# Two-part-size FFN: parts of 576, 768 and 768 tokens in place of three of 704, and the first weight blocks prepared during the out projection

## The reference

```python
def block_out(x, pool_o, attn_o, w_out, norm_ffn, w_gate, w_up, w_down):
    h = x + jnp.concatenate([pool_o, attn_o], axis=-1) @ w_out
    hn = rms_norm(h, norm_ffn)
    return h + (jax.nn.silu(hn @ w_gate) * (hn @ w_up)) @ w_down
```

## Time and profile before

| | before |
|---|---|
| median of three runs | 2101.21 us (2101.12 to 2104.17) |
| profiled execution | 2103.07 us, its span 2101.3 us |
| PE busy | 2075.9 us, 99% of the span |
| PE weight loads | 1885.5 us |
| DVE / ACT / POOL busy | 1277.1 / 884.0 / 777.9 us |
| mean granted clock of PE | 0.997 |
| DMA | 212.89 MB, mean 101 GB/s |

### The profile page before, as it was taken

One profiled execution on the slowest core, in us unless ns is written; L12 is line 12 of the kernel. 1 busy time (PEld: TensorE's weight loads), 2 busy tenths in 40 slices (PEclk: granted clock), 3 DMA queues, 4 the chain that ended last, 5 costly groups with the idle time before them and its releaser, 6 DMA issues.

```text
span 2101.3 us, 33467 instructions
## 1 busy us (share of the span) xinstructions
PE 2075.9 (99%) x12470; PEld 1885.5 (90%) x12470; DVE 1277.1 (61%) x2070; ACT 884.0 (42%) x2149; POOL 777.9 (37%) x503
## 2 busy tenths in 40 slices
PE   8999999999999999999999999999999999999999
PEld 7888888877888899999998999999998999999997
DVE  5655555553222566766666766766667767666665
ACT  6766666653334533333333433333334333333331
POOL 0000000034324544354435653445445643544352
PEclk9999999999999999999999999999999999999999
DMA  7011111033774532333224523333224422222222
GB/s 189 29 41 41 39 39 41 24 101 112 219 243 148 171 108 89 110 106 109 78 77 151 189 88 108 108 106 90 95 81 159 161 81 70 72 81 72 70 80 75
DMA packets 243401, 212.89 MB, mean 101 GB/s; under 512 B 21149, under 2 KB 220618, under 8 KB 243242
## 3 DMA queue, kind: packets, MB, share of 16 engines
q1 hardware_dynamic: 243242, 210.76, 32.6%
HBM read 170.03 MB, written 40.79 MB: 100 GB/s over the span
## 4 chain that ended last, share of the span: by engine, by line
PE 93%; ACT 2%; DVE 1%; issue 1%; SPq 1%; DMA 1%; POOL 0%; DVEq 0%; ACTq 0%; POOLq 0%
PE ps L813 27%; PE ps L815 27%; PE ps L814 27%; PE ps L914 2%; PE ps L888 2%; PE ps L1030 1%; PE ps L900 1%; PE ps L832 1%; SPq L466 1%; PE ps L1032 1%; PE ps L1028 1%; PE ps L876 1%; ACT s_sb L1208 1%; PE ps L931 1%; PE ps L940 0%
## 5 line engine op out<-in xcount | busy, mean ns | idle before, releaser
L746 POOL TENSOR_TENSOR w_lo<-w_lo_raw,w_hi 128x512 fp32r<-128x512 f32 (+1 forms) x240 | 393.3, 1645 | 606.5 <-PE ps L815 412.7
L813 PE MATMUL ps<-xs_hi,w_hi 128*128 128x352 f32 x1848 | 596.5, 323 | 3.6 <-POOL w_lo L746 2.8
L815 PE MATMUL ps<-xs_lo,w_hi 128*128 128x352 f32 x1848 | 597.8, 324 | 0.0
L813 PEld LDWEIGHTS ps<-xs_hi,w_hi 128*128 128x128 f32 x1848 | 347.6, 188 | 5.7 <-POOL w_lo L746 3.1
L815 PEld LDWEIGHTS ps<-xs_lo,w_hi 128*128 128x128 f32 x1848 | 351.0, 190 | 0.0
L1718 DVE TENSOR_TENSOR h<-ps,h 128x512 f32<-128x512 f32 (+1 forms) x396 | 270.3, 688 | 118.4 <-PE ps L815 112.1
L814 PE MATMUL ps<-xs_hi,ws_lo 128*128 128x352 f32 x1056 | 339.6, 322 | 0.0
L746 POOL TENSOR_TENSOR ws_lo<-ws_lo_raw,w_hi 128x512 fp32r<-128x512 f32 x204 | 295.3, 1449 | 112.2 <-DVE ws_lo_raw L1561 68.4
L1275 ACT ACTIVATE w_hi<-ws_lo_raw 128x512 fp32r<-128x512 f32 x264 | 165.5, 628 | 326.2 <-DVE ws_lo_raw L1561 326.0
L813 PE MATMUL ps<-w_hi,act_hi 128*128 128x512 f32 x660 | 257.2, 390 | 2.6 <-DVE act_lo L1641 2.6
L814 PE MATMUL ps<-w_hi,act_lo 128*128 128x512 f32 x660 | 256.9, 389 | 0.0
(11 more groups left out here) (142 smaller groups left out, 3248.0 us busy)
## 6 DMA issues: line engine op xcount, KB each, us to landing
w_lo_raw<-in_w_gate SPq DMA_DIRECT2D x66, 512.0 KB, 5.1
w_lo_raw<-in_w_up SPq DMA_DIRECT2D x66, 512.0 KB, 5.2
w_lo_raw<-in_w_down SPq DMA_DIRECT2D x66, 512.0 KB, 4.1
xload<-in_x_prompt SPq DMA_DIRECT2D x16, 512.0 KB, 4.2
mix_d<-o_st SPq DMA_DIRECT2D x64, 128.0 KB, 1.8
xt_lo_raw<-mix_d SPq DMA_DIRECT2D x16, 512.0 KB, 6.0
wg_hi_raw<-in_x_prompt SPq DMA_DIRECT2D x16, 512.0 KB, 5.1
h_d<-wg_hi_raw SPq DMA_DIRECT2D x16, 512.0 KB, 2.6
```

Source lines behind the costliest of these rows:

```text
L746: nc.gpsimd.tensor_tensor(lo, raw, hi.bitcast(F32), ALU.subtract).then_inc(done, 1)
L813: nc.tensor.matmul(out, s_hi, m_hi, start=first, stop=False, skip_group_check=partial)
L815: return nc.tensor.matmul(out, s_hi, m_lo, start=False, stop=final, skip_group_check=partial)
```

## The change

1. The parts are 576, 768 and 768 tokens: 4.5, 6 and 6 tiles, NB = 288, 384 and 384. Only the first part has a half tile; the last part's last tile holds 64 prompt and 64 sample rows and is stored in two transfers.
2. High and low row blocks lie in one tensor, `xs`, of 14 slots. Because of the sizes, part 0's low block 6 lies in the ends of slots 3 to 5, so that from block 3 on `rows_high(1, m)` waits for product (21, 6).
3. The high part of weight block 0, and the sum that is block 1, get a place of their own (`first_hi`, `first_s3`). `weight_sum(0, 0)`, `high2(0, 0)` and `low2(0, 0)` run at tiles 8, 9 and 10 of the out projection; `rows_high` and `first_rows_low` of part 0 run a tile earlier.
4. ACT's last step of the out projection is ordered anew, and both `stage_copy` of the last tile, with their `x_transposes` on PE, move to later: the transposes behind products (0, 4) and (0, 6) (they were behind 2 and 4), the copies behind gates 0 and 2.
5. SP issues `load_gate_up(2)` ahead of `load_down(0)` and the last `store_hn`; it was behind both.
6. At the end of part 0, `rows_low(1, 3)` and `rows_low(1, 4)` run together, since there is one tile less.

**ACT, around the end of the out projection.** Before: (`w_hi<-` rows are `high2`; `wg_lo_raw<-ps` is `stage_copy` of tile 15; the 64-row ones are the last tile's norm; `p<-ps` is `save_p1(0)`)

The diff, cut to its core:

```diff
-PARTS = 3
-T = TOKENS // PARTS
-NB = T // 2
+T_OF = (576, 768, 768)
+FIRST = (0, 576, 1344)
+PARTS = len(T_OF)
+NB_OF = tuple(n // 2 for n in T_OF)
...
+            with ExitStack() as once:
+                first_hi = sb("first_hi", [PART, HALF_K * PART], F32R, scope=once)
+                first_s3_raw, first_s3_lo = twin("first_s3", [PART, HALF_K * PART], once)
...
+            load_gate_up(2)
+            for b in range(3):
+                sp.wait_ge(h_stored[b], 16 * len(range(b, NTILES, 3)))
             load_down(0)
             store_hn(NTILES - 1)
-            for b in range(3):
-                sp.wait_ge(h_stored[b], 16 * len(range(b, NTILES, 3)))
...
+                if i == 10:
+                    low2(0, 0)
...
-            for m in range(PRODUCTS):
+            for m in range(1, PRODUCTS):
                 low2(0, m)
...
-                        if j < PT_TILES - 1:
+                        if (G // GROUPS, j) != (0, HALF_TILE):
...
                 product(0, m)
-                if m in (2, 4):
-                    x_transposes(2 * NTILES - 1, m // 2 - 1)
+                if m in (4, 6):
+                    x_transposes(2 * NTILES - 1, m // 2 - 2)
...
-                if i >= 10:
-                    rows_high(0, X_HIGHS[i - 10])
+                if i == 9:
+                    high2(0, 0)
+                if 9 <= i < 16:
+                    rows_high(0, X_HIGHS[i - 9])
+                if i == NTILES - 1:
+                    high2(0, 1)
+                    high2(0, 2)
                 stage_copy(i - 1, 0)
                 if i == NTILES - 1:
-                    for m in range(3):
-                        high2(0, m)
+                    high2(0, 3)
                 stage_copy(i - 1, 1)
-            for m in range(3, PRODUCTS):
+            for m in range(4, PRODUCTS):
                 high2(0, m)
...
                         rows_low(p + 1, j - 1)
+                        if j == HALF_TILE and TILES_OF[p] == HALF_TILE + 1:
+                            rows_low(p + 1, j)
```

More of the change, by code:

```diff
@@ L408, in part_rows, with y_stores @@
         def part_rows(p, j):
-            return (DEC if j == PT_TILES - 1 else PART), T * p + PART * j
+            return min(PART, T_OF[p] - PART * j), FIRST[p] + PART * j
         def y_rows(p, j):
             rows, a = part_rows(p, j)
-            return y_sample[0] if a == SEQ else y_prompt[0, a:a + rows, :]
+            end = min(a + rows, SEQ)
+            both = [(y_prompt[0, a:end, :], 0, end - a)]
+            return both + ([(y_sample[0], end - a, rows)] if a + rows > SEQ else [])
+        def y_stores(p, j):
+            return sum(len(y_rows(b, j)) * (1 + ((b, j) == (PARTS - 1, LAST_TILE))) for b in range(p) if j < TILES_OF[b])
         def x_step(t):
@@ L451, in rows_raw, with block_in, xs_hi, lows_of @@
                 return (turn_b, turn_a)[m][:, :, :]
-            return xs_raw[:, m]
+            return lows_of(xs_raw, p, m)
+        def block_in(t, p, slot):
+            return t[:, slot, 0:HALF_K * NB_OF[p]].rearrange("p (k n) -> p k n", k=HALF_K)
+        def xs_hi(p, m):
+            return block_in(xs_split, p, m)
+        def lows_of(t, p, m):
+            if p == 0 and m == PRODUCTS - 1:
+                return t[:, 3:3 + HALF_K, HALF_K * NB_OF[0]:(HALF_K + 1) * NB_OF[0]]
+            return block_in(t, p, PRODUCTS + m)
+        def xs_lo(p, m):
+            return lows_of(xs_split, p, m)
         def tiles_of(G):
-            return (0, 1, 2, 3, 5, 4) if G == NG - 1 else tuple(range(PT_TILES))
+            return (0, 1, 2, 3, 5, 4) if G == NG - 1 else tuple(range(TILES_OF[G // GROUPS]))
+        def d_units(G):
+            return sum(2 * TILES_OF[g // GROUPS] for g in range(G))
         def d_index(G, j, nh=0):
-            return D_UNITS * G + 2 * tiles_of(G).index(j) + nh
+            return d_units(G) + 2 * tiles_of(G).index(j) + nh
         block = ctx.enter_context(nc.Block())
@@ L760, in first_rows_low @@
                 pool.wait_ge(x_sum, 1 if m == 1 else 4)
-                low(xs_high, X_HIGHS.index(m) + 1, xs_lo[:, m], xs_raw[:, m], xs_hi[:, m], xs_split_pool)
+                low(xs_high, X_HIGHS.index(m) + 1, xs_lo(0, m), rows_raw(0, m), xs_hi(0, m), xs_split_pool)
             def mix_low(i):
@@ L1758, in _ @@
                 h_norm(i - 1)
+                if i == 8:
+                    weight_sum(0, 0)
                 if 9 <= i < 13:
                     first_rows_sum(i - 9)
-                elif i >= 13:
-                    first_rows_low(X_LOWS_DVE[i - 13])
+                if 12 <= i < 16:
+                    first_rows_low(X_LOWS_DVE[i - 12])
                 out_add(i, 0)
                 if i == NTILES - 1:
-                    for n in range(4):
+                    for n in range(1, 4):
                         weight_sum(0, n)
```

144 lines of the change are left out of this document (77 added, 67 removed).

## The result

| | before | after |
|---|---|---|
| median | 2101.22 us (20 runs) | 2105.49 us (20 runs, 2102.02 to 2108.67) |
| ratio of the runs | | 1.002, 95% interval 1.0014 to 1.0026 |
| profiled execution, its span | 2103.07, 2101.3 | 2103.69, 2101.8 |

What follows compares the result with a forecast made beforehand. PE, busy for 99% of the span, was taken as the bound. Terms 0 - 10.2 - 2.1 + 1.0 + 1.1 - 0.6 + 1.2 = -9.6 us led to a forecast of 2093 us, range 2088.5 to 2098.5.

Steps and rivals of the forecast that it cites:

- The half tiles: In down, one half and one full tile replace three half tiles: 0.93 us less in each of 11 groups, 10.2 us.
- The pitch of 288: Part 0's matmuls of 288 columns start 0.1333 us apart, on the line (columns + 32) / 2400 us.
- Product (0,0) at once: At the FFN's start, product (0,0) follows directly behind the transposes and its 2.8 us wait goes.
- a new wait of 2.4 us takes the old one's place: At the start, product (0,3) waits 2.4 us for ACT's copy of product 0, save_p1(0).
- down(10): End of part 0: waits of 2.6 us in all at down(10), 1.1 more than before.
- (22,4): Part 1's start: product (22,4) newly waits 1.2 us for u2_sum(22), 0.6 to 2.
- The start: Waits at the FFN's start fall from 4.9 to 2.8 us, a gain of 2.1 us.
- I allow 0.3 at product (2,3) (0 to 2.8): Set 2's highs and lows pass DVE, ACT and POOL in turn; product (2,3) waits 0.3 us.
- I take 0.1 us in each of ten groups: Part 0's steady groups: two chains near their end cost 1.0 us in all, with 0 and 3 as ends.
- chain (b): Part 0's steady groups: save_p1 ends 4.7 us behind the set's start, product (6,3) comes at 4.8, a tie.
- my rival for the other side: POOL becomes part 0's bound, its chain starting later: 1.3 us in each of ten groups, 2105; 7 in 100.
- I take no fall: Behind the start's new wait PE's clock does not fall; 3 chances in 10 of one costing up to 1.7 us.

Runs made afterwards that it cites:

- E11: The changed kernel as it is, measured again beside before on another chip: 2104.91 us, ratio 1.0018.
- E5: Changed kernel with ACT's copies early, also at the start, u2 ahead of row low 5, q7 and u2 ahead of the fourth low part: 2097.05 us, ratio 0.9981.
- E12: Changed kernel, its start kept, with ACT's copy early, q7 and u2 ahead of the fourth low part, u2 ahead of row low 5: 2098.9 us, ratio 0.9983.
- E4: Changed kernel with DVE's sum u2 ahead of row low 5 at a part's start: 2103.86 us, ratio 1.0006.
- E8: Changed kernel with set 2's gate load issued behind the last tile's store and the down weights again: 2109.4 us, ratio 1.0044.
- E7: Changed kernel with unused matmuls put in the waits ahead of products (0,3), (2,3) and (22,4): 2101.55 us, ratio 1.0005.
- E9: E5 plus DVE's sums q7 and u2 of set 0 ahead of the last tile's norm: 2093.88 us, ratio 0.9964.
- E3: Changed kernel with ACT's copy ahead of the fourth high part, in groups that are not a part's last: 2102.09 us, ratio 0.9998.
- E10: Changed kernel with three parts of 704, ACT's first copy ahead of the last norm, DVE's first sums ahead of its norm: 2096.28 us, ratio 0.9972.

## Why the prediction was wrong

**Right.** The half tiles: 10.2 forecast, 10.0 measured. The pitch of 288. Product (0,0) at once, and "a new wait of 2.4 us takes the old one's place": 2.7. down(10): 2.6 against 2.45. That (22,4) would wait for u2. The start was to give 2.1 us; it gave nothing: 5.7 before (I had read 4.9: the slow clock cost 1.7, not 1.3, and (1,4) 1.0), 6.0 after.

**The step that failed, first: "I allow 0.3 at product (2,3) (0 to 2.8)".** It was 2.9 by the first profile and by E11's. The 0.3 was worked out from no row: I let the chain of set 2 pass "DVE, ACT and POOL in turn" as if none of the three stretched another. In the rows above, POOL's three lows came just ahead of DVE's two-input operations, which took 1.1, 1.1 and 0.9 us longer. The Trainium skill (SBUF — State Buffer, SBUF: two separate sides) calls that port pair an exclusive lock, the first to start keeping it for its whole instruction; the pairs of rows at 716.62 and 716.67, and at 717.87 and 717.92, agree, each DVE operation ending within 0.15 us of POOL's end plus its own undisturbed duration. I had cited it for the steady groups, and not used it at set 2, where POOL starts as soon as PE's last matmul of set 1 frees its buffers (716.62) and DVE is in the middle of its pieces.

**Second: "I take 0.1 us in each of ten groups".** It was 0.28 at (2G,3) in each of the nine besides (2,3), and 0.57 more at (2G,4) in four of them in the first profile and eight in E11's: 4.8 us and 6.9. The first is my chain (b): I let the copy end 4.7 behind the set's start, 0.15 sooner than before, and it ended at 4.86. The second was not among the chains that I named: u2 on DVE, behind the fourth low part. In a steady group of the changed kernel, DVE:

```profile
793.89 0.73 DVE L1695 TENSOR_TENSOR act_hi<-aa,act_hi 128x64 fp32r<-128x64 f32 x1 [0.51 <-ACT act_hi L1370]
794.54 1.57 DVE L1697 TENSOR_TENSOR act_lo<-aa,act_hi 128x288 fp32r<-128x288 f32 x1
796.04 0.45 DVE L1654 TENSOR_TENSOR q<-ps,p 128x288 f32<-128x288 f32 x1
796.41 0.44 DVE L1659 TENSOR_TENSOR u<-ps,p 128x288 f32<-128x288 f32 x1
```

The low part at 794.54 lies on POOL's low of 794.52 to 795.80, takes 1.57, and u2 ends at 796.85; product (6,4) could have started at 796.49. In before u2 ended 6.5 behind the set's start and (2G,4) came at 7.7; now it comes at 6.4, so this chain was a tie as well. E5 and E12 put the sums ahead of the low part, and the steady groups lost nothing: that POOL's chain begins later and binds, my rival for the other side, was not it; here POOL got in first and DVE was held. That the rival's time, 2105, is the time measured is chance.

**Third, (22,4): 1.2 forecast, 2.1 measured.** I added 9% to each row low. The two that now stand together took 4.51 us instead of 3.5, with POOL's lows beside them; the first row is the changed kernel's, the second is E4's pair of row lows 5 and 6, with POOL idle:

```profile
1090.90 4.51 DVE L1647 TENSOR_TENSOR xs<-xs_raw,xs 128x1536 fp32r<-128x1536 f32 x2
...
1096.60 3.41 DVE L1647 TENSOR_TENSOR xs<-xs_raw,xs 128x1536 fp32r<-128x1536 f32 x2
```

**Fourth: "I take no fall" of the clock.** In the first profile none followed (0,3) or (2,3), but one followed (22,4), for 1.6 us, and E4, E5, E8 and E12 had one behind the start's wait. Ahead of before's wait at (0,0) PE had not only made transposes, as I wrote: its out projection ran up to 688.87 without a gap, at full clock. So what I put between the two waits does not tell them apart. Beside each other on one chip (E11), the clocks of the changed kernel and of before are 0.9975 and 0.9976, 0.3 us: not the main part of the difference. Before had its own fall behind (0,0) to give up.

The sum: 2.6 at (2,3), 0.25 at (1,4), 3.8 in steady groups, 0.9 + 1.6 at (22,4), 0.6 at down(21) and 0.3 at (0,3) are 10.1 us; 2093.5 + 10.1 is 2103.6, and the profiled execution took 2103.69. What this sum leaves out cancels: 1.0 more in the small rest, 0.2 less won by the half tiles, and 0.1 at (0,0), against 1.0 more that before had to give up (0.8 at the start, 0.2 at the two ends) and 0.15 at down(10). The median is 1.8 higher than this execution; more steady groups that wait, as in E11's profile, and more falls of the clock would do it, but no run shows which.

What stays open: how much of E7's gain is clock, why down(21) lost 1.5 and not the 0.9 forecast, and whether the sizes are worth their 2.4 us. That POOL holds DVE was read from rows that coincide, in several kernels, and from steady groups of one execution that differ in little else (E11); at (2,3) no kernel here took POOL's operation away while leaving all else.

## What to carry to other kernels

Making one engine's unit of work shorter makes every fixed chain beside it longer in comparison: list all chains that end in the shorter period, with the slack of each, and price a slack under 0.3 us as a wait (here a slack of 0.1 became a loss of 0.28). A wait that is removed at the start of a chain of in-order engines reappears at the next operation that stands behind the same late thing (here (0,0), then (0,3), then (0,4), then (1,4)), so follow it until it ends; at the start E9 needed two moves, on two engines, where one alone won nothing. Where rows show that operations of two engines stretch each other, count an operation of the second at up to the first's duration more wherever the two can meet, and give no value to a slack that rests on which of two comes first by 0.02 us.

## What the runs showed of the hardware

DVE operations with two inputs in SBUF took 0.22 us (64 columns) and 0.46 (288) alone, and 1.32 and 1.57 when POOL's 1.30 us operation had started 0.05 us before them. Where POOL's started 16 to 27 ns ahead of DVE's, either DVE's took 1.57 and POOL's 1.28, or DVE's 0.45 and POOL's 1.61, from group to group of one execution. PE's clock fell to 1.2 GHz behind some waits of 2 to 3 us and not behind others of the same kernel and length (behind (22,4) in the first profile, not in E11's; behind (0,3) in E4, E8 and E12, not in E3); when the same waits were filled with matmuls it stood at 1.00 behind all three, as in E11's profile without them. The lowest clock was that of the kernel with the longest waits (E8, 0.9952), the highest those of E9 and E10 (0.9988).
